# A pooling, recurrence and attention model on one core: heads turned as transposes with backward reads, and four places with waits put in another order

## The reference, cut to what matters

```python
def first_block(x, norm_g, pool_w_in, ..., final_g):
    h = x
    for layer in range(DEPTH):                       # 2 layers
        hn = rms_norm(h, norm_g[layer])
        ...
            y = pool_mixer(hn, pool_w_in[j], pool_w_grp[j], pool_scale[j], pool_w_out[j])
        ...
            y = hgrn2_mixer(hn, hgrn_w_in[j], lbs[layer], hgrn_norm_g[j], hgrn_w_out[j])
        h = h + y.astype(h.dtype)
    return rms_norm(h, final_g)
```

```python
    o = o * lax.rsqrt(jnp.mean(o * o, axis=-1, keepdims=True) + EPS)
    o = (o * norm_g.astype(jnp.float32).reshape(HGRN_HEADS, HGRN_HEAD_DIM)).reshape(B, T, D_INNER)
    return (o * jax.nn.silu(gate)) @ w_out
```

```python
        x = x + mod_l[2] * y
        h2 = _modulate(_rmsnorm(x, norm2_g[l]), mod_l[3], mod_l[4])
        x = x + mod_l[5] * _conv_ffn(h2, ffn_w_up[l], ffn_conv_w[l], ffn_conv_b[l], ffn_w_down[l])
    return _rmsnorm(x, final_norm_g)
```

## Time and profile before

| | us |
|---|---|
| three runs | 823.28, 822.31, 825.67 |
| median | 823.28 |
| the profiled execution, its own time | 822.8 |
| its span in the trace | 821.6 |
| granted TensorE clock, mean | 0.999 |
| busy: PE, PEld | 805.2, 691.5 |
| busy: DVE, ACT, POOL | 626.3, 472.7, 40.2 |
| read from HBM, written | 156.02 MB, 3.21 MB |

### The profile page before, as it was taken

How to read it: one execution, slowest core, us unless ns; L and a number is a source line. 1 busy time by engine, 2 the same in 40 slices (tenths; PEclk the granted TensorE clock), 3 DMA queues, 4 the chain that set the end, 5 groups by cost and what they waited for, 6 DMA issues and landing times.

```text
span 821.6 us, 12747 instructions
## 1 busy us (share of the span) xinstructions
PE 805.2 (98%) x5099; PEld 691.5 (84%) x5099; DVE 626.3 (76%) x922; ACT 472.7 (58%) x794; POOL 40.2 (5%) x52
## 2 busy tenths in 40 slices
PE   8999999999999999999999999998999999999996
PEld 6999998878988999999988789985476888888885
DVE  6786687646799889799795885998749877767775
ACT  6564454446577768858856551646636654554443
POOL 6000003600000000000000000000000000000000
PEclk9999999999999999999999999999999999999999
DMA  8879975784644444456356772935637555655631
GB/s 282 309 258 262 264 250 206 238 291 137 204 119 139 148 138 130 150 155 205 110 163 231 268 259 89 371 137 180 227 151 238 197 174 187 205 173 186 206 103 51
DMA packets 105701, 160.05 MB, mean 195 GB/s; under 512 B 11317, under 2 KB 74137, under 8 KB 103338
## 3 DMA queue, kind: packets, MB, share of 16 engines
q1 hardware_dynamic: 105642, 159.24, 59.3%
HBM read 156.02 MB, written 3.21 MB: 194 GB/s over the span
## 4 chain that ended last, share of the span: by engine, by line
PE 87%; DVE 7%; ACT 3%; DMA 2%; issue 1%; SPq 0%; DVEq 0%; ACTq 0%
PE acc L459 9%; PE acc L461 9%; PE acc L460 9%; PE acc L480 9%; PE acc L511 8%; PE acc L512 8%; PE acc L513 8%; PE acc L481 4%; PE misc L1306 3%; PE misc L2302 2%; PE misc L2304 2%; PE misc L2303 2%; PE misc L907 2%; PE acc L484 1%; DVE w_lo L432 1%
## 5 line engine op out<-in xcount | busy, mean ns | idle before, releaser
L432 DVE TENSOR_TENSOR w_lo<-raw,w_hi 128x2048 fp32r<-128x2048 f32 x114 | 263.2, 2320 | 60.0 <-ACT w_hi L425 59.9
L425 ACT ACTIVATE w_hi<-raw 128x2048 fp32r<-128x2048 f32 x114 | 217.5, 1911 | 69.3 <-PE acc L513 21.4
L459 PE MATMUL acc<-X,w_hi 128*128 128x256 f32 x592 | 168.8, 285 | 0.8 <-DVE sg L1175 0.8
L461 PE MATMUL acc<-X,w_lo 128*128 128x256 f32 x592 | 167.5, 283 | 0.0
L460 PE MATMUL acc<-X,w_hi 128*128 128x256 f32 x592 | 167.4, 283 | 0.0
L459 PEld LDWEIGHTS acc<-X,w_hi 128*128 128x128 f32 x592 | 113.5, 192 | 5.4 <-issue 2.6
L460 PEld LDWEIGHTS acc<-X,w_hi 128*128 128x128 f32 x592 | 113.5, 192 | 0.3
L461 PEld LDWEIGHTS acc<-X,w_lo 128*128 128x128 f32 x592 | 113.5, 192 | 0.0
L480 PE MATMUL acc<-X,w_hi 128*128 128x512 f32 x308 | 110.3, 397 | 0.8 <-DVE X L656 0.8
L481 PE MATMUL acc<-X,w_lo 128*128 128x256 f32 x308 | 86.3, 280 | 0.0
L511 PE MATMUL acc<-w_hi,X 128*128 128x512 f32 (+1 forms) x176 | 69.1, 393 | 0.9 <-DVE w_lo L432 0.5
(11 more groups left out here) (302 smaller groups left out, 1496.1 us busy)
## 6 DMA issues: line engine op xcount, KB each, us to landing
raw<-in_hgrn_w_in_dram SPq DMA_DIRECT2D x32, 1024.0 KB, 5.7
ada_raw<-in_ada_w_dram SPq DMA_DIRECT2D x24, 1024.0 KB, 7.2
raw<-in_ffn_w_up_dram SPq DMA_DIRECT2D x22, 1024.0 KB, 5.0
raw<-in_pool_w_in_dram SPq DMA_DIRECT2D x15, 1024.0 KB, 6.8
raw<-in_ffn_w_down_dram SPq DMA_DIRECT2D x11, 1024.0 KB, 4.9
raw<-in_w_in_dram SPq DMA_DIRECT2D x10, 1024.0 KB, 6.1
raw<-in_pool_w_out_dram SPq DMA_DIRECT2D x8, 1024.0 KB, 5.1
raw<-in_hgrn_w_out_dram SPq DMA_DIRECT2D x8, 1024.0 KB, 5.0
```

The lines of the kernel that those rows point to most:

```text
L425: self.hi_done.up(act.activation(self.w_hi[v % RING][:, 0:w], self.raw[j][:, 0:w], ACT.Copy), v)
L432: self.lo_done.up(dve.tensor_tensor(self.w_lo[j][:, 0:w], self.raw[j][:, 0:w], self.w_hi[v % RING][:, 0:w].bitcast(F32), ALU.subtract), v)
L459: pe.matmul(o, wh[:, k, c:c + P], xh[:, k, :], start=k == 0, stop=False)
L461: m = pe.matmul(o, wl[:, k, c:c + P], xh[:, k, :], start=False, stop=k == K - 1)
```

## The change

It has five parts.

1. **The start.** `hi(1)` and `lo(1)` are split in two halves (`hi_part`, `lo_part`). ScalarE's first half stands ahead of the reads of the second token half; VectorE does both halves one behind the other where `lo(1)` was. `pe_idle(6)` becomes `pe_idle(2)`.
2. **The heads.** The four matmuls of `pe_turn_heads` become four transposes, all against the plain identity, with the two heads' first halves in one half of the bank and their second halves in the other. The reads of the second halves go backward through PSUM. Each 128x256 read becomes two of 128x128, on ScalarE and on VectorE.
3. **The attention.** In step 1 `pe_ada(14)` stands ahead of `pe_turn_e(1)`; the two `dve_mix` go behind `dve_normalize(4)` and `dve_normalize(6)`.
4. **The feed-forward part.** `dve_ada(3)` goes ahead of the second half's `dve_low`, and the row of the end gate is spread ahead of `pe_up(0)`, into banks 0 and 3.
5. **The end.** VectorE starts on the second half of the tokens before it has scaled the first; both halves' scaling stands later, on VectorE behind the last `dve_times`, on ScalarE between the second half's two sums of squares.

```diff
+    def hi_part(self, v, i):
+        act, c = self.nc.scalar, slice(i * UNIT // 2, i * UNIT // 2 + UNIT // 2)
+        act.wait_ge(self.raw_in[v].h, self.raw_in[v][v])
+        ins = act.activation(self.w_hi[v][:, c], self.raw[v][:, c], ACT.Copy)
+        self.hi_done.up(ins, *(("part", v) if i == 0 else (v,)))
+
+    def lo_part(self, v, i):
+        dve, c = self.nc.vector, slice(i * UNIT // 2, i * UNIT // 2 + UNIT // 2)
+        dve.wait_ge(self.hi_done.h, self.hi_done["part", v] if i == 0 else self.hi_done[v])
+        ins = dve.tensor_tensor(self.w_lo[v][:, c], self.raw[v][:, c], self.w_hi[v][:, c].bitcast(F32), ALU.subtract)
+        self.lo_done.up(ins, *(("part", v) if i == 0 else (v,)))
...
-        self.lo(1)
+        for i in range(2):
+            self.lo_part(1, i)
...
             self.hi_piece(half)
+            if half:
+                self.hi_part(1, 0)
             for c in range(2):
                 self.act_high("x", half, c, self.XH)
-        self.hi(1)
+        self.hi_part(1, 1)
         self.hi(2)
...
-        self.pe_idle(6)
+        self.pe_idle(2)
...
-        for h in range(2):
-            for half in range(2):
-                turn = view(self.ident, P - 1, (-1, P)) if half else self.ident[:, :]
-                m = pe.matmul(bank[:, h * TOK + half * P:h * TOK + half * P + P],
-                              self.SG[:, half, (2 * r + h) * P:(2 * r + h) * P + P], turn, start=True, stop=True)
+        for half in range(2):
+            for h in range(2):
+                m = pe.transpose(bank[:, half * TOK + h * P:half * TOK + h * P + P],
+                                 self.SG[:, half, (2 * r + h) * P:(2 * r + h) * P + P], self.ident[:, :])
         self.T.up(m, "heads", q, r)
 
+    def heads_turned(self, q, r, h, half):
+
+        bank, c = self.turn_bank(q, r), half * TOK + h * P
+        return view(bank, c + P - 1, (-1, P)) if half else bank[:, c:c + P]
...
-            self.A.up(act.activation(self.MHb[:, n, :], bank[:, h * TOK:h * TOK + TOK], ACT.Copy,
-                                     scale=self.param("hgrn_norm_g", n)), "mb_hi", q, r)
+            for half in range(2):
+                self.A.up(act.activation(self.MHb[:, n, half * P:half * P + P], self.heads_turned(q, r, h, half), ACT.Copy,
+                                         scale=self.param("hgrn_norm_g", n)), "mb_hi", q, r)
...
+            for half in range(2):
+                t = slice(half * P, half * P + P)
+                self.V.up(dve.scalar_tensor_tensor(out=self.MLb[:, n, t], in0=self.heads_turned(q, r, h, half),
...
+            if s == 1:
+
+                self.pe_ada(self.ADA_BESIDE[s][0])
             self.pe_turn_e(s)
-            for a in self.ADA_BESIDE[s]:
+            for a in self.ADA_BESIDE[s] if s != 1 else ():
                 self.pe_ada(a)
...
         self.dve_softmax(1)
-        self.dve_mix("mix_conv", 6, self.CA)
-        self.dve_mix("mix_gate", 4, self.U)
...
             self.dve_normalize(s)
+            if s == 4:
+                self.dve_mix("mix_conv", 6, self.CA)
+            if s == 6:
+                self.dve_mix("mix_gate", 4, self.U)
...
+        self.dve_ada(3)
         for c in range(2):
             self.dve_low("ffn", 1, c, self.XH, self.XL)
         self.lo(self.first(u0, 1) + RING)
-        self.dve_ada(3)
...
+        self.pe_last_rows("end_gate", 3, (0, 3))
         self.pe_up(0)
-        self.pe_last_rows("end_gate", 3, (0, 1))
...
                 self.act_square("end", half, self.x_tok[:, half, c * 512:c * 512 + 512], self.XN3[:, half, c * 512:c * 512 + 512], c)
+                if half and c == 0:
+                    self.act_last_scale(0)
             self.act_root("end", half, 2)
...
+        self.act_last_scale(1)
```

More of the change, by code:

```diff
@@ L1419, in act_heads_high @@
             n = 4 * q + 2 * r + h
-            self.A.up(act.activation(self.MHb[:, n, :], bank[:, h * TOK:h * TOK + TOK], ACT.Copy,
-                                     scale=self.param("hgrn_norm_g", n)), "mb_hi", q, r)
+            for half in range(2):
+                self.A.up(act.activation(self.MHb[:, n, half * P:half * P + P], self.heads_turned(q, r, h, half), ACT.Copy,
+                                         scale=self.param("hgrn_norm_g", n)), "mb_hi", q, r)
     def dve_heads_low(self, q, r):
-        dve, bank = self.nc.vector, self.turn_bank(q, r)
+        dve = self.nc.vector
         dve.wait_ge(self.A.h, self.A["mb_hi", q, r])
@@ L1427, in dve_heads_low @@
             n = 4 * q + 2 * r + h
-            self.V.up(dve.scalar_tensor_tensor(out=self.MLb[:, n, :], in0=bank[:, h * TOK:h * TOK + TOK],
-                                               scalar=self.param("hgrn_norm_g", n), in1=self.MHb[:, n, :].bitcast(F32),
-                                               op0=ALU.mult, op1=ALU.subtract), "mb_lo", q, r)
+            for half in range(2):
+                t = slice(half * P, half * P + P)
+                self.V.up(dve.scalar_tensor_tensor(out=self.MLb[:, n, t], in0=self.heads_turned(q, r, h, half),
+                                                   scalar=self.param("hgrn_norm_g", n),
+                                                   in1=self.MHb[:, n, t].bitcast(F32),
+                                                   op0=ALU.mult, op1=ALU.subtract), "mb_lo", q, r)
     def level_dims(self, l, block, row, token):
@@ L2345, in act_ffn @@
                 for c in range(2):
-                    A.up(act.activation(self.e_row[:, c * 512:c * 512 + 512], self.misc[c][:, :], ACT.Copy), "e_row")
+                    A.up(act.activation(self.e_row[:, c * 512:c * 512 + 512], self.misc[3 * c][:, :], ACT.Copy), "e_row")
             for f in range(2):
@@ L2404, in act_end, with act_last_scale @@
                 self.act_square("end", half, self.x_tok[:, half, c * 512:c * 512 + 512], self.XN3[:, half, c * 512:c * 512 + 512], c)
+                if half and c == 0:
+                    self.act_last_scale(0)
             self.act_root("end", half, 2)
-            act.wait_ge(self.V.h, self.V["rstd", "end", half])
-            act.wait_ge(self.V.h, self.V["times", "end", half, 1])
-            y = self.Y[:, half, 512:D]
-            self.A.up(act.activation(y, y, ACT.Copy, scale=self.nstat[:, half, 4:5]), "scaled", "end", half)
+        self.act_last_scale(1)
+    def act_last_scale(self, half):
+        act, y = self.nc.scalar, self.Y[:, half, 512:D]
+        act.wait_ge(self.V.h, self.V["rstd", "end", half])
+        act.wait_ge(self.V.h, self.V["times", "end", half, 1])
+        self.A.up(act.activation(y, y, ACT.Copy, scale=self.nstat[:, half, 4:5]), "scaled", "end", half)
     def dve_last_sum(self, half, c):
@@ L2418, in dve_last_sum, with dve_last_scale @@
         dve.wait_ge(V.h, t)
+    def dve_last_scale(self, half):
+        y = self.Y[:, half, 0:512]
+        self.V.up(self.nc.vector.tensor_scalar(y, y, self.nstat[:, half, 4:5], None, ALU.mult), "scaled", "end", half)
     def dve_end(self):
-        dve, V = self.nc.vector, self.V
+        dve, row = self.nc.vector, self.last_row
         dve.wait_ge(self.gain_in["end"].h, self.gain_in["end"]["all"])
-        for half in range(2):
-            self.dve_last_sum(half, 0)
-            self.dve_times("end", half, 0, self.last_row)
-            self.dve_last_sum(half, 1)
-            self.dve_part("end", half)
-            self.dve_times("end", half, 1, self.last_row)
-            self.dve_root("end", half)
-            y = self.Y[:, half, 0:512]
-            V.up(dve.tensor_scalar(y, y, self.nstat[:, half, 4:5], None, ALU.mult), "scaled", "end", half)
+        self.dve_last_sum(0, 0)
+        self.dve_times("end", 0, 0, row)
+        self.dve_last_sum(0, 1)
+        self.dve_part("end", 0)
+        self.dve_times("end", 0, 1, row)
+        self.dve_last_sum(1, 0)
+        self.dve_root("end", 0)
+        self.dve_times("end", 1, 0, row)
+        self.dve_last_sum(1, 1)
+        self.dve_part("end", 1)
+        self.dve_times("end", 1, 1, row)
+        self.dve_last_scale(0)
+        self.dve_root("end", 1)
+        self.dve_last_scale(1)
     def sp_end(self):
```

2 lines of the change are left out of this document (1 added, 1 removed).

## The result

| | before | the change |
|---|---|---|
| median of 16 runs, us | 825.25 | 821.90 |
| lowest and highest | 822.31, 828.23 | 818.80, 823.23 |
| profiled execution, span | 821.6 | 819.9 |
| mean granted clock of that execution | 0.999 | 0.997 |

The ratio is 0.9949, with an interval of 0.9933 to 0.9964: 4.2 us faster by the ratio, 3.35 by the medians. The forecast was 817.4 us, which is 0.9929 of the 823.28 it started from, and a range up to 820.6. The measured time lies over that range. Two things stand in the distance: the median of before was 2.0 us higher over 16 runs than over the three shown, and the gain was smaller than the 5.85 of the sum.

What follows compares the result with a forecast made beforehand. PE (TensorE) was taken as the bound, its work 87% of the chain at full clock. Terms -0.5 - 3.5 - 1.2 - 0.95 + 0.3 = -5.85 took 823.28 to 817.4 us, range 815.7 to 820.6.

Steps and rivals of the forecast that it cites:

- start: Unit 1's preparation in halves: PE goes on at 20.0 to 20.1 us, saving 0.5 us; bounds -0.55 to +2.5.
- heads: Heads' turns: 64 records become 32 of equal length, -3.6 us, less 0.1 for waits on ScalarE: -3.5 us.
- attention: Attention step 1: VectorE's chain loses two dve_mix, saving 1.2 us of PE's 1.99 wait; bounds -1.0 and -2.0.
- feed-forward: Entrance of the feed-forward part: the gate's row moves into idle time before pe_up(0), -0.95 us; bounds -0.9 and -1.05.
- end: Last scaling starts 0.38 us earlier, but all four stores run in one block: +0.3 us; bounds -0.4 and +0.6.
- sum: Whole kernel: the five terms together give -5.85 us, taken from 823.28 us to 817.4 us.
- the step behind the sum: Looking in the timeline only at places the change touches, for PE's idle times and what ends them.
- the stores don't stack up: First rival, at the end: stores keep up, so the end gives -0.4 and the time is 816.7 us; chance 0.15.
- the clock steps up later at the start: Second rival: matmuls after 14.59 us run partly or wholly at the lower clock, giving 818.8 or 820.4 us; chance 0.28.
- the heads give less, or wait for ScalarE: Third rival: shorter saving and waits for ScalarE or VectorE take about half of 3.5 us, giving 819.1; chance 0.10.
- Two records for a transpose: Fourth rival, heads' turns: a transpose takes two records as the matmul did, no 3.5 saved, 820.9 us; chance 0.02.
- Backward reads that stall: Fifth rival, heads: backward PSUM reads costing 2 us more each make PE wait 11.6 us, giving 829.0; chance 0.03.

Runs made afterwards that it cites:

- e14: The change with three pairs of small transfers and two modulation loads moved, first-half scaling moved back, and pe_idle(6), against the kernel before: ratio 0.9864, median 814.76 us.
- e15: The change with small transfers and two modulation loads moved, first-half scaling moved back, and the old start, against the kernel before: ratio 0.9874, median 815.54 us.
- e3: Only the attention and feed-forward parts (third and fourth) put on the kernel before, against that kernel: ratio 0.9953, median 822.07 us.
- e5: The whole change again, unaltered, against the kernel before on the same chip: ratio 0.9918, median 821.22 us.
- e6: The change without its first part, so with the old start, against the kernel before: ratio 0.9936, median 822.25 us.
- e10: The change with VectorE's scaling of the first half moved back ahead of its product of quarter (1, 0), against the kernel before: ratio 0.9897, median 818.03 us.
- e8: The change with two 1 MB modulation weight loads issued at about 490 us in place of 507, against the kernel before: ratio 0.9887, median 818.09 us.
- e9: The change with six idle stretches at the start, pe_idle(6), as before, against the kernel before: ratio 0.9891, median 817.68 us.
- e1: Only the first part (halves of unit 1, two idle stretches) put on the kernel before, against that kernel: ratio 1.0005, median 826.82 us.
- e2: Only the second part (heads turned as transposes, backward reads) put on the kernel before, against that kernel: ratio 0.9959, median 822.52 us.
- e4: Only the fifth part (the end's scalings later) put on the kernel before, against that kernel: ratio 1.0009, median 827.02 us.
- e7: The change with three pairs of small BIAS transfers issued behind unit 19, at 116 us and later, against the kernel before: ratio 0.9878, median 817.85 us.
- e11: The kernel before with only the three pairs of small BIAS transfers moved behind unit 19, against the kernel before: ratio 0.9964, median 823.24 us.

## Why the prediction was wrong, and where it was right

**The terms of the sum.** By the positions in the traces:

| | forecast | in its place |
|---|---|---|
| start | -0.5 | -0.72 (after); -0.78 in time (e14, e15) |
| heads | -3.5 | -3.6 |
| attention | -1.2 | -1.2 |
| feed-forward | -0.95 | -0.97 (e3) |
| end | +0.3 | +0.34 (0.43 less before the last scaling, 0.77 more behind it) |
| sum | -5.85 | -6.15 |

The start's lower bound, -0.55, was too tight: the forecast let unit 1 begin only when L855's busy time is over, at 20.03, and it begins at 19.84, while that time still runs.

**What failed is the step behind the sum**, "I looked, in the timeline, at each place that the change touches". PE's waits elsewhere were not read. One stood in the trace of before, 0.78 us at 107 for weights that were 8.15 us on their way, in a stretch whose DMA share was full. So the forecast put at nothing, without a reason, the term that sets the time from run to run: a wait of nothing to 3.4 us, and 1.4 more where the clock falls behind it, 4.8 at most, where its range leaves 3.2 above the forecast. It missed three things by it. First, the median of three executions, 823.28, was no base to 0.5 us: over 16 it was 825.25, and the ratio forecast, 0.9929, would have been 819.4 of that. Second, a gain can be covered: the first measurement has 4.2 us of the 6.15, the second, e5, has 6.8. Third, and small, 0.2 to 1.2 us are given back at 525, which was not in the sum.

The two profiles add up with these terms: -6.15, +2.3 for the longer wait at 107, +1.4 for the clock behind it, +1.2 at 525 and -0.3 for the kernel before's own wait at 186 give -1.6, and the spans differ by 1.6 (821.57, 819.94). For the other runs of the first measurement only the mean granted clock is known, not the places. A fall takes 0.002 off it, and in all 17 profiles the clock is also low at the very end, where no matmul is left (0.7 to 4.6 us, up to 0.003 off). So 0.995 or less, in 11 of the 16 runs, means at least one fall, and 0.994 or less, in five of them, at least two, where the profiled one has one.

Whether the change itself makes the late landing at 107 more frequent stays open: it was long in after, e6 and e10 (whole or nearly whole change) and short or nothing in e5, e8 and e9 (the same up to there) as in before, e1, e2, e3 and e4. Those are too few executions for a share. The runs' mean granted clocks (how they are read is said above) don't settle it either: they are 0.995 or less in 3, 2 and 2 of the six runs of e5, e6 and e8, for 7 of 11 of the kernel before on their chip, and in one of six of e9 and of e10, for 3 of 15 on theirs. No way to bring the late landing about at will was found.

**The rivals.** That the stores don't stack up: false, they do. That the clock steps up later at the start: false in after. Its weight loads take 0.33 us up to 12.34, and behind the hole four take 0.42, where four at 7.76 took 0.71:

```profile
12.34 0.33 PEld L526 LDWEIGHTS acc<-w_hi,X 128*128 128x128 f32 x1
14.61 0.42 PEld L650 LDWEIGHTS misc<-ident,XN 128*128 128x128 f32 x4 [1.94 <-DVE w_lo L415]
```

It can fall again, as in one of eight profiles with that start, e7's, at some 1.5 us. The forecast leaned on the page's clock column, which is full in the first slice; but a window of 9 to 13 us of the kernel before gives 1.00 as well, where its loads take 0.33 us. So at the start it is the loads' own times that show the clock, and the column does not. That the heads give less, or wait for ScalarE: false, no wait appears with the margin of 0.1 us. Two records for a transpose: false. Backward reads that stall: false; the four reads of a step take 1.1 us, as four forward ones of 0.28 would.

**The rule on transposes.** The Trainium skill, "TensorE: Matmul & The Clock Gate", section "Terms", calls the transpose mode four times as fast for fp32. The trace doesn't agree for this use: 8 steps save 0.45 each, half of the 0.9 that eight records took, which is the two-to-one of the earlier trace rows.

**The attention's wait was worth more than its length.** e3, which removes it, is faster by 3.9 us (ratio 0.9953, interval 0.9931 to 0.9975) for 2.2 by position. In the profiles with the wait of 1.99 (before, e1, e2, e4, e11) the clock fell behind it in two, e1 and e11, at some 1.5 us each. In the twelve with 0.83 in its place it never did. e11's runs show how often: eight of the ten lie at 823.2 to 823.6 us with a mean granted clock of 0.996 or 0.997, the profiled one with its fall among them, and two at 821.9 and 822.3 with 0.998 and 0.999. So by times and clock it seems to fall in eight of ten, 1.1 us or so on average. This accounts for part of e3's 1.7 us; the interval holds the rest.

## What to carry to other kernels

List every wait of the bounding engine first, also outside the places that a change touches, and for each one that ends with a transfer ask how the transfer's time varies; a few us of such a wait hide or fake a change of 0.5%. Take one source of the spread away (here three pairs of small transfers beside the weight loads) before terms under 1 us are timed: the same comparison that could not be told in 2.2 us of spread was plain in 0.1. A wait of TensorE can cost more than its length where the clock falls behind it, so taking a wait of 2 us away may give more than the chain shows.

## What the runs showed of the hardware

**The clock falls behind waits, not always.** By the granted clock in windows of 4 us, it was at its lower level for about 3 us behind PE's idle times of 3.1 (after), 2.6 (e6) and 3.4 us (e10) at 107, in three of three; behind 1.99 to 2.02 us in three profiles (e1, e7, e11) and not in three others (before, e2, e4); and in no profile behind the shorter ones, of 0.5 to 1.3 us at 107 and up to 1.95 us at the start. Each fall cost 1.4 to 1.5 us.

**A backward read of PSUM costs nothing here**, on ScalarE or VectorE, in tiles of 128x128 as in 128x512. VectorE's 32 reads of the heads, half of them backward, take 341 to 352 ns; for 128x512 see the earlier trace rows.

**A 1 MB weight load takes 5 to 10.8 us** from issue to landing (4.9 is the median of the ffn_w_down loads in after, 10.8 the longest before the wait at 107, in e10). The one issued at 93 to 95 us took 7.8 to 10.8 with the small transfers beside it, by the profiles in which PE waited for it, and 6.7 without (e7).
